# Seven quarter products instead of eight for the feed-forward up and gate projections

## What is computed

```python
def swiglu(h, w1, w3, w2):
    return (jax.nn.silu(h @ w1) * (h @ w3)) @ w2
    x = x + 0.5 * swiglu(rmsnorm(x, ffn1_norm[l]), ffn1_w1[l], ffn1_w3[l], ffn1_w2[l])
    ...
    x = x + 0.5 * swiglu(rmsnorm(x, ffn2_norm[l]), ffn2_w1[l], ffn2_w3[l], ffn2_w2[l])
```

## Time and profile before

| | |
|---|---|
| runs | 2985.59, 2987.79, 2988.18 us |
| span of the profiled execution | 2985.6 us |
| busy | PE 2956.7, PEld (weight loads) 2426.5, DVE 1661.0, ACT 1134.2, POOL 71.8 us |
| granted TensorE clock | 9 tenths or more in all 40 slices |

### The profile page before, as it was taken

The page is one execution under the profiler, slowest core; times in us unless marked ns, Lnnn a source line. Parts: engine busy times, 40 slices in busy tenths (PEclk is TensorE's granted clock), DMA queues, the critical chain, the costliest instruction groups (busy, mean ns, idle before and its releaser), DMA issues.

```text
span 2985.6 us, 33257 instructions
## 1 busy us (share of the span) xinstructions
PE 2956.7 (99%) x14146; PEld 2426.5 (81%) x14146; DVE 1661.0 (56%) x1901; ACT 1134.2 (38%) x1357; POOL 71.8 (2%) x84
## 2 busy tenths in 40 slices
...
DMA packets 41923, 270.52 MB, mean 91 GB/s; under 512 B 5776, under 2 KB 6032, under 8 KB 10544
## 3 DMA queue, kind: packets, MB, share of 16 engines
...
## 4 chain that ended last, share of the span: by engine, by line
PE 87%; DVE 6%; ACT 5%; issue 1%; DVEq 0%; POOL 0%; DMA 0%; ACTq 0%; SPq 0%; POOLq 0%
PE PS L257 26%; PE PS L259 26%; PE PS L258 26%; DVE w_lo L231 3%; ACT w_hi L223 3%; DVE XT L1566 2%; PE PS L2187 1%; PE PS L635 1%; PE PS L1155 1%; PE PS L1183 1%; PE PS L694 0%; PE PS L996 0%; PE PS L2167 0%; PE PS L2168 0%; ACT SP L741 0%
## 5 line engine op out<-in xcount | busy, mean ns | idle before, releaser
L223 ACT ACTIVATE w_hi<-w_raw 128x2048 fp32r<-128x2048 f32 x241 | 461.2, 1914 | 1125.6 <-PE PS L259 1125.4
L231 DVE TENSOR_TENSOR w_lo<-w_raw,w_hi 128x2048 fp32r<-128x2048 f32 x239 | 547.7, 2292 | 383.0 <-ACT w_hi L223 382.0
L257 PE MATMUL PS<-uh_b,w_hi 128*128 128x512 f32 x1312 | 511.7, 390 | 0.0
L259 PE MATMUL PS<-uh_b,w_lo 128*128 128x512 f32 x1312 | 510.6, 389 | 0.0
L258 PE MATMUL PS<-ul_b,w_hi 128*128 128x512 f32 x1312 | 510.5, 389 | 0.0
L257 PE MATMUL PS<-uh_a,w_hi 128*128 128x512 f32 x864 | 339.6, 393 | 1.1 <-DVE ul_a L583 0.7
L258 PE MATMUL PS<-ul_a,w_hi 128*128 128x512 f32 x864 | 336.4, 389 | 0.0
L259 PE MATMUL PS<-uh_a,w_lo 128*128 128x512 f32 x864 | 336.4, 389 | 0.0
L259 PEld LDWEIGHTS PS<-uh_b,w_lo 128*128 128x128 f32 x1312 | 246.3, 188 | 51.4
L258 PEld LDWEIGHTS PS<-ul_b,w_hi 128*128 128x128 f32 x1312 | 246.3, 188 | 50.8
L257 PEld LDWEIGHTS PS<-uh_b,w_hi 128*128 128x128 f32 x1312 | 246.3, 188 | 50.7
...
## 6 DMA issues: line engine op xcount, KB each, us to landing
w_raw<-in_weights SPq DMA_DIRECT2D x241, 1024.0 KB, 4.8
...
mem_raw<-in_mem SPq DMA_DIRECT2D x2, 1024.0 KB, 4.9
...
```

The source lines that it names most:

```text
L223: act.activation(self.hi[g % 2][:], self.raw[g % 2][:], ACT.Copy).then_inc(self.hi_done.sem, 1)
L231: dve.tensor_tensor(self.lo[g % 2][:], self.raw[g % 2][:], self.hi[g % 2][:], ALU.subtract).then_inc(self.lo_done.sem, 1)
L257: pe.matmul(out, sh, mh, start=first, stop=False)
L259: return pe.matmul(out, sl, mh, start=False, stop=last)
```

## The change

In chunks 1 to 10 of each of the four stages the up block and the gate block are computed by a scheme of seven products of quarters instead of eight. A block's weights (1024 by 256) are cut into four quarters of 512 inputs by 128 features, the activations (1024 by 512 tokens) into four quarters of 512 inputs by 256 tokens. With sums of quarters on both sides, seven products of 128 features by 256 tokens over 512 inputs suffice, each 12 matmuls of 256 columns (`product`, `paired`): 84 matmuls of 256 columns for a block instead of 48 of 512. Chunk 0 and the down blocks are as before.

What it adds: four sums of weight quarters per block on GpSimd (`Weights.sums`, one of them written over the raw quarter a21, three into a single buffer S); three more quarters to split (`hi_first` and `lo_first` for the three raw quarters, `hi_rest` and `lo_rest` for the three sums and the fourth); one copy out of PSUM on ACT (`first_copy`); six reads of 128x256 on DVE per block in place of one of 128x1024, and multiplies by R or the weighed up product for what these sums left (`first_sums`, `first_quarter`, `last_sums`). Both blocks now use banks 0 to 3. Products a12, a22 and s4 are accumulated onto banks whose first sum has been read. At the start of a stage the activations are multiplied by the norm's gain into `xg` (eight ACT steps), four combinations of 128x1024 are formed (T 0 and 1 on GpSimd, T 2 and 3 on DVE) and split (`t_high` on ACT, `t_low` on DVE).

Beside it the masks of the recurrence are sent as bytes and no longer converted on DVE (one step of 128x2304), some buffers are placed elsewhere, and semaphores of other stages are used again under joined names (`heads_v_out_ff_reads` and the like).

```diff
+    def sums(self, pool, g, free):
+        raw = self.raw[g % 2]
+        a12, a11, a22, a21 = (raw[:, j * 512:(j + 1) * 512] for j in range(4))
+        s3, s2, s4 = (self.S[:, j * 512:(j + 1) * 512] for j in range(3))
+        pool.wait_ge(*self.loaded[g % 2].at(16 * (g // 2 + g % 2)))
+        pool.wait_ge(*free)
+        pool.tensor_tensor(s3, a11, a21, ALU.add)
+        pool.drain()
+        pool.tensor_tensor(a21, a22, a21, ALU.add)
+        pool.drain()
+        pool.tensor_tensor(s2, a21, a11, ALU.add)
+        pool.drain()
+        pool.tensor_tensor(s4, s2, a12, ALU.add).then_inc(self.summed.sem, 1)
+    def hi_first(self, act, g):
+        assert g == self.hi_next, g
+        self.hi_next += 1
+        act.wait_ge(*self.loaded[g % 2].at(16 * (g // 2 + g % 2)))
+        act.wait_ge(*self.used.at(g - 1))
+        act.activation(self.hi[g % 2][:, 0:1536], self.raw[g % 2][:, 0:1536], ACT.Copy).then_inc(self.hi_first_done.sem, 1)
+    def hi_rest(self, act, g):
+        act.wait_ge(*self.summed.at(self.paired[g] + 1))
+        act.activation(self.hi2[g % 2][:], self.S[:], ACT.Copy)
+        act.activation(self.hi[g % 2][:, 1536:], self.raw[g % 2][:, 1536:], ACT.Copy).then_inc(self.hi_done.sem, 1)
+    def lo_first(self, dve, g):
+        assert g == self.lo_next, g
+        self.lo_next += 1
+        dve.wait_ge(*self.hi_first_done.at(self.paired[g] + 1))
+        dve.tensor_tensor(self.lo[g % 2][:, 0:1536], self.raw[g % 2][:, 0:1536], self.hi[g % 2][:, 0:1536], ALU.subtract)\
+           .then_inc(self.lo_first_done.sem, 1)
+    def lo_rest(self, dve, g):
+        dve.wait_ge(*self.hi_done.at(g + 1))
+        dve.tensor_tensor(self.lo2[g % 2][:], self.S[:], self.hi2[g % 2][:], ALU.subtract)
+        dve.tensor_tensor(self.lo[g % 2][:, 1536:], self.raw[g % 2][:, 1536:], self.hi[g % 2][:, 1536:], ALU.subtract)\
+           .then_inc(self.lo_done.sem, 1)
...
+    B11, B12, B21, B22 = ((slice(4 * kh, 4 * kh + 4), slice(256 * th, 256 * th + 256)) for kh in range(2) for th in range(2))
+    def gained_part(self, at):
+        return self.m.xg[:, at[0], at[1]]
+    def gpsimd(self, pool):
+        w, T = self.k.w, self.T
+        pool.wait_ge(*self.gained.at(4))
+        pool.tensor_tensor(T.wide[:, 0], self.gained_part(self.B11), self.gained_part(self.B12), ALU.subtract).then_inc(self.t_pool.sem, 1)
+        pool.wait_ge(*self.gained.at(KD))
+        pool.tensor_tensor(T.wide[:, 1], self.gained_part(self.B12), self.gained_part(self.B22), ALU.subtract).then_inc(self.t_pool.sem, 1)
+        for c in range(1, NCHUNK):
+            w.sums(pool, self.up(c), w.lo_done.at(self.gate(c - 1) + 1) if c > 1 else self.rows.summed.at(1))
+            w.sums(pool, self.gate(c), w.lo_done.at(self.up(c) + 1))
...
+        def gained(c):
+            if c == 0:
+                act.wait_ge(*self.incoming.x.at(KD))
+                act.wait_ge(*w.used.at(self.g0))
+            act.activation(m.xg[:, c, :], k.XT[:, c, :], ACT.Copy, scale=self.incoming.gain(c)).then_inc(self.gained.sem, 1)
+        def t_high(i):
+            act.wait_ge(*(self.t_pool.at(i + 1) if i < 2 else self.t_dve.at(i - 1)))
+            act.activation(T.hi[:, i], T.wide[:, i], ACT.Copy).then_inc(self.t_hi.sem, 1)
...
+        def first_copy(n, to, free):
+            act.wait_ge(*free)
+            act.wait_ge(*self.products.at(6 * n + 1))
+            act.activation(to[:, 1, 0:256], k.PS[:, 0, 0:256], ACT.Copy).then_inc(self.first_copied.sem, 1)
+        for c in range(4):
+            gained(c)
         w.split_hi(act, self.g0 + 1)
+        for c in range(4, KD):
+            gained(c)
+        t_high(0)
+        t_high(1)
+        w.hi_first(act, self.g0 + 2)
+        t_high(2)
         self.rows.root(act)
-        w.split_hi(act, self.g0 + 2)
+        t_high(3)
         self.rows.row(act)
+        w.hi_rest(act, self.g0 + 2)
         silu(0)
         for c in range(1, NCHUNK):
-            w.split_hi(act, self.up(c) + 1)
+            w.hi_first(act, self.gate(c))
+            first_copy(2 * c - 2, m.a, self.gated.at(c))
+            w.hi_rest(act, self.gate(c))
             if c == 1:
                 high(0)
-            w.split_hi(act, self.gate(c) + 1)
+            w.split_hi(act, self.down(c - 1))
+            first_copy(2 * c - 1, m.h, self.h_lo.at(c))
             silu(c)
-            w.split_hi(act, self.down(c - 1) + 1)
+            if c + 1 < NCHUNK:
+                w.hi_first(act, self.up(c + 1))
+                w.hi_rest(act, self.up(c + 1))
+            else:
+                w.split_hi(act, self.down(c))
...
+        def first_sums(n, to):
+            dve.wait_ge(*self.first_copied.at(n + 1))
+            dve.wait_ge(*self.products.at(6 * n + 2))
+            dve.tensor_tensor(to[:, 0, 256:512], bank[1], to[:, 1, 0:256], ALU.subtract).then_inc(self.reads.sem, 1)
+            dve.drain()
+            dve.wait_ge(*self.products.at(6 * n + 3))
+            dve.tensor_tensor(to[:, 1, 256:512], bank[2], to[:, 0, 256:512], ALU.add).then_inc(self.reads.sem, 1)
+            dve.drain()
+            dve.wait_ge(*self.products.at(6 * n + 4))
+            dve.tensor_tensor(to[:, 1, 256:512], to[:, 1, 256:512], bank[3], ALU.subtract).then_inc(self.reads.sem, 1)
+        def first_quarter(n, to, by):
+            dve.wait_ge(*self.products.at(6 * n + 5))
+            dve.tensor_tensor(to[:, 0, 0:256], bank[0], by, ALU.mult).then_inc(self.reads.sem, 1)
+        def last_sums(n, g, to):
+            dve.wait_ge(*self.products.at(6 * n + 6))
+            dve.tensor_tensor(to[:, 1, 0:256], bank[2], to[:, 0, 256:512], ALU.add).then_inc(self.reads.sem, 1)
+            w.wait_used(dve, g)
+            dve.drain()
+            dve.tensor_tensor(to[:, 0, 256:512], bank[3], to[:, 0, 256:512], ALU.subtract).then_inc(self.reads.sem, 1)
+            dve.drain()
...
+        dve.wait_ge(*self.t_pool.at(1))
+        dve.wait_ge(*self.gained.at(KD))
+        dve.tensor_tensor(T.wide[:, 2], self.gained_part(self.B22), T.wide[:, 0], ALU.add).then_inc(self.t_dve.sem, 1)
+        dve.drain()
+        dve.tensor_tensor(T.wide[:, 3], self.gained_part(self.B21), T.wide[:, 2], ALU.subtract).then_inc(self.t_dve.sem, 1)
+        t_low(0)
         self.rows.mean(dve)
+        t_low(1)
         self.rows.refine(dve)
-        w.split_lo(dve, self.g0 + 2)
+        w.lo_first(dve, self.g0 + 2)
+        t_low(2)
         dve.wait_ge(*self.rows.row_ready.at(1))
-        scale(0)
+        w.wait_used(dve, self.up(0))
+        dve.tensor_tensor(m.a[:], k.PS[:, 0:2, :], R, ALU.mult).then_inc(self.scaled.sem, 1)
+        t_low(3)
+        w.lo_rest(dve, self.g0 + 2)
         weigh(0)
         for c in range(1, NCHUNK):
+            up, gate = 2 * c - 2, 2 * c - 1
             if c == 1:
-                gate(0)
+                w.wait_used(dve, self.gate(0))
+                dve.wait_ge(*self.weighed.at(1))
+                dve.tensor_tensor(m.h[:], k.PS[:, 4:6, :], m.a[:], ALU.mult).then_inc(self.gated.sem, 1)
             else:
                 add(c - 2, 3)
-            w.split_lo(dve, self.up(c) + 1)
+            w.lo_first(dve, self.gate(c))
             if c == 1:
                 low(0)
-            scale(c)
-            w.split_lo(dve, self.gate(c) + 1)
-            weigh(c)
+            first_sums(up, m.a)
+            w.lo_rest(dve, self.gate(c))
+            first_quarter(up, m.a, k.R[:, 0:256])
+            last_sums(up, self.up(c), m.a)
+            dve.tensor_tensor(m.a[:, 0, 256:512], m.a[:, 0, 256:512], k.R[:, 256:512], ALU.mult)
+            dve.tensor_tensor(m.a[:, 1, :], m.a[:, 1, :], k.R[:], ALU.mult)
+            dve.drain()
+            dve.sem_inc(self.scaled.sem, 1)
+            w.split_lo(dve, self.down(c - 1))
             if self.aside and c == 8:
                 self.aside.take(dve)
-            gate(c)
-            w.split_lo(dve, self.down(c - 1) + 1)
-            add(c - 1, 0)
+            first_sums(gate, m.h)
+            weigh(c)
+            dve.drain()
+            first_quarter(gate, m.h, m.a[:, 0, 0:256])
+            last_sums(gate, self.gate(c), m.h)
+            flat = [x[:].rearrange("p a n -> p (a n)")[:, 256:1024] for x in (m.h, m.a)]
+            dve.tensor_tensor(flat[0], flat[0], flat[1], ALU.mult).then_inc(self.gated.sem, 1)
+            if c + 1 < NCHUNK:
+                w.lo_first(dve, self.up(c + 1))
+                add(c - 1, 0)
+                w.lo_rest(dve, self.up(c + 1))
+            else:
+                w.split_lo(dve, self.down(c))
+                add(c - 1, 0)
             add(c - 1, 1)
             low(c)
             add(c - 1, 2)
...
+        def product(g, name, moving, bank, fresh):
+            for j in range(4):
+                i = split_products(pe, k.PS[:, bank, 0:256], w.operand(g, name, j), moving(j), fresh and j == 0, j == 3, not fresh)
+            return i
+        def raw(at):
+            return lambda j: [x[:, at[0].start + j, at[1]] for x in self.u]
+        def combined(i):
```

(41 more changed lines are left out.)

104 lines of the change are left out of this document (69 added, 35 removed).

## The result

| | before | changed |
|---|---|---|
| median of 20 runs each | 2987.83 us | 2991.07 us |
| lowest, highest | 2985.59, 2988.7 | 2989.5, 2994.48 |
| span of the profiled execution | 2985.6 | 2988.1 |

The ratio is 1.0014 (95%: 1.0007 to 1.002). The forecast was 2971.5, so the kernel is 19.6 us slower than forecast. The stated range held the time, but the direction was wrong: a gain of 0.5% was forecast, and a small loss was measured.

The account below looks back on a forecast made before the run. PE, busy 99% of the span, was taken as the bound: -73.5 us in the loop and +57.2 in the stage openings gave -16.3, so span 2969.3 and median 2971.5 us; range 2944 to 3003.

Parts of the forecast that it names:

- The pace and the chunk: Feed-forward loop: 256-column matmuls 0.120 us apart, chunks 31.0 to 31.2 us, saving 73.5 us together.
- POOL's price: GpSimd's sums of weight quarters: a step of 512 columns was taken at 1.29 us, between 0.73 and 1.45.
- Turns: DVE and POOL steps on SBUF tiles: each waits for the other but for 0.12 us at a step's end.
- Rival 1: Stage openings: no turns between DVE and POOL, so openings cost 35.2 us and the time is 2949.5; chance 0.25.
- The openings: Start of each stage: PE waits 15.4, 11.4, 19.0 and 11.4 us, 57.2 in all.
- a22 waited: Up block of chunk 1: PE waits 7.2 us per stage for first_sums, behind POOL's four sums.
- The turn: The norm's turn on PE, 19.3 us into a stage: waits 3.2 in stage one, 6.8 in three.
- ahead of a11: Stage opening: PE waits for scale of chunk 0, behind t_low(2); 2.0 us, 2.8 in stages one and three.
- s2: Product in the stage opening: PE waits 2.0 us for lo_rest of up(1), behind t_low(3).
- "The last chunk, the masks and the buffers change nothing": These were costed at nothing on PE's path, as lying beside PE's 99%; the dropped mask conversion was some 2.5 us of DVE.
- +57.2: Sum in us of PE's forecast waits in the four stage openings; without turns 35.2.
- Rival 2: Loop: DVE becomes the bound, deciding from some 1.5 us per POOL sum; 3013 us at 1.6; chance 0.16.

Follow-up runs that it names:

- The run with the norm first: Changed kernel with the norm's root moved up on ACT, and mean and refine ahead of the low parts on DVE: 2990.32 us against 2986.83 before the change.
- The last run: Changed kernel with 31 result-less matmuls ahead of a22 of up(1) per stage and Floors spread over chunks 2 to 9: 2970.56 us against 2986.88 before the change.
- the unused matmuls: Changed kernel with 31 matmuls whose result nobody reads, ahead of a22 of up(1) in each stage: alone 2985.65 us against 2986.63 before the change.

## Why the prediction was wrong

- **The pace and the chunk** were right: 0.120 a step, 31.15 to 31.17 us a chunk (31.0 to 31.2 forecast), 74.8 us for 73.5.
- **POOL's price**, 1.29, is what the rows show alone. By the Trainium skill's figure (GPSIMD Engine Reference, section 3.1) it would have been the estimated 1.12; the trace has 1.26 to 1.30.
- **Turns** were right for large steps: at 1542.85 a sum takes 3.39. DVE's low split of 2.29 had begun at 1542.79, so 1.29 + 2.29 less that 0.06 and the 0.12 of the prediction is 3.40.

```profile
1542.85 3.39 POOL L195 TENSOR_TENSOR w_S<-w_raw 128x512 f32<-128x512 f32 x1 [12.62 <-DMA w_raw<-in_weights]
```

  Rival 1, no turns, falls. By the exclusive lock that the Trainium skill states (SBUF — State Buffer, "SBUF: two separate sides") the estimate is 3.52; the row is 0.13 shorter.
- **The openings**: 12.7, 11.5, 17.1 and 11.5 us read, 15.4, 11.4, 19.0 and 11.4 forecast. a22 waited 6.8 to 7.4 (7.2 forecast) and the gate block 0.3 (0.2). The turn waited 5.6, 1.9, 8.0 and 1.9 instead of 3.2, 0, 6.8 and 0, and in return nothing waited ahead of a11 (2.0 to 2.8 forecast). The run with the norm first kept the sum of these waits. So the sum was near, but its parts were not: the turn was too cheap by 7.4 us over the stages, a11 and s2 too dear.
- **"The last chunk, the masks and the buffers change nothing"**, and with them I costed everything that shared DVE at nothing. This step failed: DVE's chunk was added up from the steps that the diff shows, 25.0 us, and `Floors`, which the diff doesn't touch, was left out. DVE had 16 us of slack per chunk before and 6 now. `Floors` costs 12.6 by the rows, and spreading it gave 13.3.
- **The waits were priced at their length.** The second failed step: +57.2 took PE to go on at its pace. Behind each long wait the clock was at half for another 3 to 6 us, 11.1 us by the rows.
- **Rival 2** was not taken seriously enough. It gave 1.5 us a sum as the point of decision. A sum alone costs 1.29 and 0.14 to the next one, 1.43; with the turns the eight take 12.8 us a chunk. The loop holds at that, but a ninth and a tenth sum cost 1.1 us per chunk.

Together the two failed steps are 23.7 us; the openings and the loop, dearer in the forecast than in the rows by 4.4 and 1.3, give 5.7 of it back. That is 18.0 of the 19.6 us; 0.8 lies between the account and the spans, and the rest in the medians. The last run agrees with this account to 1.1 us, and its half clock behind the turns is what the unused matmuls didn't reach.
